# A paged-attention and convolution decoder layer: cache pages by indexed gathers, convolution taps on two other engines, half of the modulation moved behind the sample loop

## The reference, cut to what matters

```
mod = silu(c) @ w_ada + b_ada                 # 6 groups of 1024: sh1 sc1 gt1 sh2 sc2 gt2
h = rms_norm(x, g_norm1) * (1 + sc1) + sh1
q, k, v, glu_a, glu_b, gate_a, gate_c = split(h @ w_in)
q, k = rms_norm(q), rms_norm(k)               # per head
# each query: the 3 past blocks of 256 keys with the largest q . mean(k), and its own block
attn = moba_attention(q, [k_past, k], [v_past, v]) @ w_attn_proj
u = glu_a * sigmoid(glu_b)
cv = depthwise_conv([conv_past, u], w_dwconv) + b_dwconv     # 31 taps, 512 channels
cv = silu(layer_norm(cv)) @ w_conv_proj
x = x + gt1 * ((sigmoid(gate_a) * attn + sigmoid(gate_c) * cv) @ w_out)
h2 = rms_norm(x, g_norm2) * (1 + sc2) + sh2
y = x + gt2 * ((silu(f_g) * f_u) @ w_ffn_out),  f_g, f_u = split(h2 @ w_ffn_in)
```

## Time and profile before

| | |
|---|---|
| time, median of 3 runs | 642.4 us (642.4, 643.26, 638.41) |
| span of the profiled execution | 639.2 us |
| PE busy | 547.9 us, 86% |
| DVE busy | 459.7 us, 72% |
| ACT busy | 191.0 us, 30% |
| POOL busy | 84.0 us, 13% |
| DMA | 159.32 MB, mean 249 GB/s |
| the chain that ended last | PE 56%, DVE 30%, DMA 9% |

### The profile page before, as it was taken

One profiled execution on the slowest core, in us unless ns is written; L12 is line 12 of the kernel. 1 busy time (PEld: TensorE's weight loads), 2 busy tenths in 40 slices (PEclk: granted clock), 3 DMA queues, 4 the chain that ended last, 5 costly groups with the idle time before them and its releaser, 6 DMA issues.

```text
span 639.2 us, 11366 instructions
## 1 busy us (share of the span) xinstructions
PE 547.9 (86%) x4000; PEld 449.8 (70%) x4000; DVE 459.7 (72%) x851; ACT 191.0 (30%) x315; POOL 84.0 (13%) x176
## 2 busy tenths in 40 slices
PE   5779998685959597879758979978999999999997
PEld 3656676453545355555526678967999999999997
DVE  3325795999997999999997579866566656655541
ACT  1102213303030303030312455337444444433341
POOL 8101400022222222223222000000000000000000
PEclk9879999799888988979888989996999999999999
DMA  9998895498999899999949995542547455366600
GB/s 293 381 387 298 271 303 213 142 311 323 336 386 342 305 316 386 368 328 328 373 168 368 334 339 211 171 132 91 174 151 232 146 188 167 92 182 181 181 35 35
DMA packets 112234, 159.32 MB, mean 249 GB/s; under 512 B 6173, under 2 KB 67658, under 8 KB 112169
## 3 DMA queue, kind: packets, MB, share of 16 engines
q1 hardware_dynamic: 100722, 122.76, 58.3%
q0 software_dynamic: 10752, 34.16, 14.9%
q10 hardware_dynamic: 703, 1.67, 0.7%
HBM read 156.33 MB, written 2.72 MB: 249 GB/s over the span
## 4 chain that ended last, share of the span: by engine, by line
PE 56%; DVE 30%; DMA 9%; issue 2%; SPq 1%; ACT 1%; DVEq 0%; ACTq 0%
PE acc L1319 13%; PE acc L1320 12%; PE acc L1321 12%; PE acc L1134 11%; DVE prod L727 7%; DVE sall L734 7%; DMA wring<-in_w_ada 6%; DVE cvT L772 5%; DMA wring<-in_w_in 2%; PE acc L1101 1%; PE chain L1276 1%; DMA wring<-in_w_conv_proj 1%; PE acc L1092 1%; DVE wlo L972 1%; PE chain L1289 1%
## 5 line engine op out<-in xcount | busy, mean ns | idle before, releaser
L1134 PE MATMUL acc<-hT,wring 128*128 128x264 f32 x576 | 158.6, 429 | 3.7 <-DMA wring<-in_w_in 2.6
L972 DVE TENSOR_TENSOR wlo<-wring,whi 128x1024 fp32r<-128x1024 f32 (+2 forms) x92 | 101.8, 1108 | 70.2 <-ACT whi L449 69.0
L1134 PEld LDWEIGHTS acc<-hT,wring 128*128 128x128 f32 x576 | 116.3, 210 | 40.2 <-issue 15.8
L1319 PE MATMUL acc<-xlo,whi 128*128 128x264 f32 x416 | 122.6, 295 | 6.5 <-DVE xlo L978 5.9
L1320 PE MATMUL acc<-xhi,wlo 128*128 128x264 f32 x416 | 119.7, 288 | 0.0
L1321 PE MATMUL acc<-xhi,whi 128*128 128x264 f32 x416 | 119.6, 288 | 0.0
L449 ACT ACTIVATE whi<-wring 128x1024 fp32r<-128x1024 f32 (+2 forms) x92 | 88.6, 965 | 93.6 <-PE acc L1321 91.3
L271 POOL DMA_DIRECT2D vring<-in_cache_v x128 | 68.8, 537 | 257.7 <-PE chain L1276 140.2
L1319 PEld LDWEIGHTS acc<-xlo,whi 128*128 128x128 f32 x416 | 80.0, 192 | 9.1 <-issue 5.7
L1320 PEld LDWEIGHTS acc<-xhi,wlo 128*128 128x128 f32 x416 | 80.3, 193 | 0.2
L727 DVE TENSOR_TENSOR prod<-kring,qbc 128x1024 f32<-128x1024 f32 x64 | 77.2, 1206 | 3.8 <-PE qbc L1155 3.2
(11 more groups left out here) (200 smaller groups left out, 500.7 us busy)
## 6 DMA issues: line engine op xcount, KB each, us to landing
kring<-in_cache_k SPq DMA_DIRECT2D x128, 256.0 KB, 5.6
vring<-in_cache_v POOLq DMA_DIRECT2D x128, 256.0 KB, 6.1
wring<-in_w_ada SPq DMA_DIRECT2D x24, 1024.0 KB, 12.6
wring<-in_w_ffn_in SPq DMA_DIRECT2D x22, 1024.0 KB, 7.0
wring<-in_w_in SPq DMA_DIRECT2D x12, 1024.0 KB, 8.4
wring<-in_w_ffn_out SPq DMA_DIRECT2D x16, 704.0 KB, 6.0
wring<-in_w_in SPq DMA_DIRECT2D x12, 512.0 KB, 8.7
wring<-in_w_out SPq DMA_DIRECT2D x4, 1024.0 KB, 9.6
```

What stands on the lines that cost most here:

```text
L972: v.tensor_tensor(wlo[:, place, 0:n, :], w, whi[:, place, 0:n, :].bitcast(F32), ALU.subtract)\
L1134: ins = mm(bank[:, 0:R], w[:, k, P * t:P * t + P], src[:, k, :], start=k == 0, stop=k == KD - 1)
L1319: mm(bank[:, 0:R], whi[:, place, k - k0, :], lo[:, k, :], start=k == 0, stop=False)
```

## The change

**Pages.** The page-wise loads are gone from SP and POOL. POOL issues indexed gathers of 1 MB instead, 32 for K and 32 for V: partition p takes 4 rows (8 KB in one piece) of the page and row that `rowof` names. A partition so holds neighbouring keys of one page and not the same key of four pages, and the distances, the block sums (`halves`, `upper`) and `pen` are made for that layout; `diag` and `pen` become twice as wide. The first 12 gathers (K and V of sample 0, K of sample 1; 12.6 MB) are issued together when `ada3` has landed (`w_full[0] >= 64`); the others between POOL's additions.

**Taps.** For each tap ACT writes a product into `cprod`, a ring of 5 (`tap_products`), and POOL adds it to `cvT` (`add_taps`). There are 20 a loop iteration for b = 0 to 5, in parts of 6, 6 and 8, so that the convolution is complete in b = 6. Its sums and centring move to b = 6, its variance to b = 7, and `scale_rows` behind the loop. Tiles a1 and b1 are computed before the loop, a2 to b3 in the loop until b = 4.

**Modulation.** The loop holds no chunk. Chunks 4 to 7 are computed behind units 5, 11, 15 and 19, chunks 8 and 9 in the norm behind `o7`, chunks 10 and 11 behind units 31 and 39 (`f7` and `f15`). `SLOTS` follows.

```
-SLOTS = (["ada0", "ada1", "ada2", "ada3", "q", "k", "v", "glu"]
-         + ["mix0", "mod4", "mix1", "mix2", "mod5", "mix3", "mix4", "mod6", "mix5", "mix6", "mod7", "mix7"]
-         + ["mod8", "mod9", "mod10", "mod11", "conv", "attn", "out0", "out1"]
+SLOTS = (["ada0", "ada1", "ada2", "ada3", "q", "k", "v", "glu"] + [f"mix{n}" for n in range(B)]
+         + ["conv", "mod4", "attn", "mod5", "mod6", "out0", "mod7", "out1", "mod8", "mod9"]
+         + ["fin0", "fin1", "mod10", "fin2", "fin3", "mod11"] + [f"fin{n}" for n in range(4, FT // 2)]
...
+ADA_AFTER = {5: 4, 11: 5, 15: 6, 19: 7, FIRST_FFN + 7: 10, FIRST_FFN + 15: 11}
+ADT_AFTER = {7: 4, 13: 5, 17: 6, 21: 7, FIRST_FFN + 9: 10, FIRST_FFN + 17: 11}
...
+CONV_RING = 5
+CONV_LOOPS = 6
+CONV_PART = CT * (TAPS - 1) // CONV_LOOPS
+CONV_SPLIT = (6, 6, 8)
...
-        def load_pages(eng, ring, cache, full, b, c):
-
-            for g in range(PC * c, PC * c + PC):
-                page = eng.value_load(pages[0:1, bass.ds(PG * b + g, 1)], min_val=0, max_val=NPHYS - 1)
-                eng.dma_start(ring[:, g, :], cache[bass.ds(page, 1)].rearrange("o p h d -> p (o h d)"))\
-                    .then_inc(full[c], 16)
...
+            def gather(ring, cache, full, b, c):
+
+                g.indirect_dma_start(
+                    out=ring[:, PC * c:PC * c + PC, :].rearrange("p j n -> p (j n)"), out_offset=None,
+                    in_=cache.rearrange("n (r j) h d -> (n r) (j h d)", j=PC),
+                    in_offset=bass.IndirectOffsetOnAxis(ap=rowof[:, b, c:c + 1], axis=0)).then_inc(full[c], 16)
...
+            def add_taps(b, part):
+
+                for i in conv_part(b, part):
+                    t = i // (TAPS - 1)
+                    pool.wait_ge(prod_ready, i + 1)
+                    if i >= 1:
+                        pool.wait_ge(conv_added, i)
+                    g.tensor_tensor(cvT[:, t, 0:S], cvT[:, t, 0:S], cprod[:, i % CONV_RING, :], ALU.add)\
+                        .then_inc(conv_added, 1)
+
+            pool.wait_ge(rows_ready, 4)
+            pool.wait_ge(acc_full, NUMBER["vec"] + 1)
+            pool.wait_ge(w_full[0], 64)
+            for c in range(CH):
+                gather_k(0, c)
+            for c in range(CH):
+                gather_v(0, c)
+            for c in range(CH):
+                gather_k(1, c)
             for b in range(B):
...
+                for part in range(3):
+                    add_taps(b, part)
+                    if b + 2 < B:
+                        gather_k(b + 2, part)
+                if b + 1 < B:
+                    for c in range(CH):
+                        gather_v(b + 1, c)
+                if b + 2 < B:
+                    gather_k(b + 2, 3)
...
+            def tap_products(b, part):
+
+                for i in conv_part(b, part):
+                    t, n = i // (TAPS - 1), 1 + i % (TAPS - 1)
...
+                    if i >= CONV_RING:
+                        act.wait_ge(conv_added, i - CONV_RING + 1)
+                    func(cprod[:, i % CONV_RING, :], u[:, t, n:n + S], ACT.Copy, scale=taps[:, n, t:t + 1])\
+                        .then_inc(prod_ready, 1)
...
-                tap()
                 multiply_next(3)
-                tap(TAPS if b == B - 1 else 1)
                 add_up_next(3)
-                if b == B - 1:
-                    samples_convolution()
-                tap()
...
+            modulation(8)
             square_sum(KD - 1)
+            modulation(9)
+            mod_turned(8)
+            mod_turned(9)
```

351 lines of the change are left out of this document (168 added, 183 removed).

## The result

The changed kernel takes 684.3 us (682.84 to 687.03, 4 runs) beside 641.65 us of the kernel before: 1.0649 times, 95% interval 1.0592 to 1.0706. Forecast were 661 us and a range of 638 to 684, whose upper end it passes by 0.3. The profiled execution has a span of 685.3 us, 46.1 more than before, with a mean granted clock of 0.90 instead of 0.93.

What follows compares the result with a forecast made beforehand. DVE was taken to bound the sample loop, with DMA also full, and PE and DVE close behind it. Terms +8 + 7.5 - 18 - 7 + 28 = +18.5 on a 639.2 span made 657.7; 3.2 under the median gave 661 us, range 638 to 684.

Steps and rivals of the forecast that it cites:

- part 4's slots: Units from cp0 on: late weight slots make PE wait 5.2, 1.4 and 6.4 us, within a term of +28.
- The norm: Norm behind the output projection: chunks 8 and 9 and `norm_scale` ahead of the reciprocal add 3.4 us.
- The loop: Iterations b = 0 to 6: 28.8 us for four, 27.8 for two, 32.9 for the last; -18 in all.
- my 5 us: Iteration b = 6: the convolution's centring, small operations and a wait for the sums add 5 us.
- The tail: From b = 7 to the first unit: 33 us instead of 40.2, so -7.
- Before the loop: Pages and projections ahead of the loop: +8 for late q beside the gathers, +7.5 for two tiles, +15.5.
- The tiles: Tiles a1 and b1 ahead of the loop: 7.36 us of PE with no engine's work beside it, +7.5.
- the lower end: Before the loop: q's missing weights come at about 170 GB/s beside the gathers, the delay's low case, +4.
- (a): Before the loop: queue turns of four times the size delay q by 16 us, not 8: 669 us, chance 0.20.
- (b): Loop: POOL becomes the bound, 36 us in each of six iterations: +45, 706 us, chance 0.10.
- (c): Loop: iterations fall to DVE's 25.6 us: 638 us, or 626 with the units' ring waits hidden; chance 0.17.
- (d): Loop: DVE and POOL hinder one another and nothing is left of the loop's gain: 679 us, chance 0.08.

Runs made afterwards that it cites:

- e1: Changed kernel with another order of weight slots, chunks and unit weights alternating, chunk 4 between the loop and cp0: 659.2 us, 1.0234.
- e4: Changed kernel without the taps' products on ACT and additions on POOL: 681.7 us, one run.
- e13: Changed kernel with e6's, e7's and e12's edits, chunks 4 to 8 in the loop, 9 and 10 ahead of cp0, 11 in the feed-forward part: 644.7 us.
- e9: Kernel of e7 with the page table's transfer on ACT's queue instead of SP's, ahead of the weights: 686.6 us, one run.
- e12: Changed kernel with the page table loaded once into one partition and spread to 128 by a matmul: 684.1 us, one run.
- e6: Changed kernel with the first gathers issued when k's weights have landed, not when chunk 3 has: 679.8 us, one run.
- e15: Kernel of e13 with chunk 8 at the head of iteration 7 instead of in iteration 6: 640.4 us, 0.9996.
- e16: Kernel of e15 with tiles a1 and b1 in iteration 0 instead of ahead of the loop: 640.3 us, 0.9985.
- e7: Changed kernel with the operations that make the list of rows placed behind DVE's copies of x: 683.7 us, one run.

## Why the prediction was wrong

**The step that failed is part 4's slots.** "ap7 waits 5.2 [...] `out1` waits for chunk 6: +1.4 [...] `fin0` [...] stops o7: +6.4" named the right three loads and the right mechanism (e1 removes some 24 us by the order), and took each wait too short: 8.04, 4.41 and 10.59, 23.0 instead of 13.0. (They stand ahead of ap6, o2 and o6: a turned chunk takes a bank between, which the prediction had left out.) o7 ends 90.8 us after cp0's start and not 74. `out0`'s slot was free at t0 + 25.7, not 23.7, as cp0 started at a granted clock of 0.50. `out1` had waited for chunk 6, which itself came behind the first wait. For `fin0` I took 7.5 us to land, and it took 14.0, as chunk 9's 2 MB stood right ahead of it on the same queue. The other 7 of the 17 us are a term that the sum did not have: PE runs at a lower clock after each long wait, 0.85 over the stretch where e1 has 0.95, and is busy some 6 us longer for the same matmuls. The norm came near its term, +4.0 instead of +3.4.

**The loop** was forecast at 28.8 and 27.8 us and takes 28.4 to 29.4 in its middle; most of the miss is at its ends, 2.3 us in iteration 0 and 2.8 in iteration 6. The failed step is that the taps cost nothing once they leave DVE ("ACT adds 20 products of some 0.35 to 6 us of 31: hidden"). A product takes 0.50, DVE's two-input operations slow down beside the additions, and e4 gives the taps 6.2 us of the loop, 2.5 of it in iteration 0. In iteration 6 PE waits 4.66 us for ppad behind the centring, the mean clock is 0.72, and the values' product takes 6.23 instead of 3.64; neither the wait nor the clock was in my 5 us.

**The tail** was sized at 33 and is 34.4 to 36.6 in six profiles. Its cover was right: PE idles 8.21 us ahead of cp0, where e13 hides two chunks.

**Before the loop** the sum (15.5, measured 14.2) came out near by luck. The late q had been put down to gathers that share the engines. They were issued at 36.7, 3 us after I had them, and did not delay q: its weights and chunk 3 were late by the table's transfer in their queue, which the sum did not have (e9, e12), and chunk 3 ran at the low clock. q lost 3.2 us so and not 8, and the gathers cost k 2.7 (e6), for which I had nothing. The tiles cost more than they should, 9.1 instead of 7.4. One sum was wrong too: 1.55 MB at 170 GB/s are 9.1 us instead of 4.0, which makes the lower end +5 and not +4.

**The rivals.** (a): q1's share beside the gathers is 29% of the bytes, between the third that I took and the fifth of this rival, but it does not decide, as q's weights did not wait for the gathers. The rule of the Trainium skill, DMA: Bandwidth & Descriptors, Queues, rings and completion order, is that an engine takes a whole packet from each queue in turn. The profile counts 828 packets of some 7.4 KB on q0 and 1246 of 2.0 KB on q1. The page's packet holds several descriptors, and no run here shows how many of the profile's make one, so the trace neither confirms nor refutes the rule; the even count of the earlier trace rows did not carry over. (b) fell: a gather's 1.25 and an addition's 0.86 make 27 us in an iteration of 28.5, closer than thought, but POOL is busy only 21.63 of them, and inside iteration 1 it waits for ACT's products (0.86 and 1.93 us), not they for it. (c) fell, iterations stay above 28. (d) is right in kind and too large in size. DVE's multiply, with its query in PSUM, is spared, as the prediction said: 1210 ns on average and 1206 before. But the operations with both inputs in SBUF slow down beside the additions, `ppad` from 284 to 486 ns in the median and up to 606, and e4 takes the cost away. It is some 5 us of DVE's time in six iterations, where (d) gave away the whole gain of 18. The trace so agrees with the rule of the Trainium skill, GPSIMD Engine Reference, Specifications, that POOL shares its way to SBUF with DVE and the two contend when a DVE instruction has two SBUF inputs.

**Did the idea fail?** Freed of its slot order, its table and its late chunks, the changed kernel is level with the kernel before (e15, e16), no better. By e15's stages the loop gives 9.7 us and the tail 4.3, and they pay for 11.1 before the loop (the two tiles, the gathers and their list), 0.9 in the units and 3.3 behind them, where chunk 11 stands. I found no version that is clearly faster than the kernel before.

## What to carry to other kernels

In a ring of few slots the price of an insertion is not its bytes but whose slot the next load takes over: write down for each load its predecessor, when that is read for the last time, and add the landing time as it is *beside the traffic of that stage* (7.5 us in one stage, 22.7 in another). If the sum is later than the consumer, reorder, so that what is read once and what is held long alternate. An engine that prefetches ahead of its own work stops everything behind it when the prefetch is late, and PE pays for a long stop again with a slow start (cp0's first 25 matmuls at a clock of 0.50). And work taken from a bound engine shortens the loop only down to the chain between the engines: 5.9 us of taps an iteration left DVE for 2.5 us of period. It is not free on the engines it moves to either: POOL's additions made DVE's two-input operations slower.

## What the runs showed that I had not expected

- 64 KB (128 pieces of the same 512 bytes) in front of the weights on SP's queue cost the weights 1.5 us of all 16 engines' work; the same transfer on ACT's queue cost them nothing (e9).
- POOL's additions of 128x256 stretched DVE's 128x128 product of two SBUF inputs from 284 to 486 ns in the median, and left its 128x1024 multiply with one input in PSUM alone.
- A queue that held pages for 32 partitions of 8 KB each, and weights, moved 183 GB/s at a share of 84.6%, where pages on 128 partitions moved at 387.
- A gather of 1 MB with one index per partition costs POOL 0.95 us, 1.25 to the next, not much more than a plain page's 0.54 and 1.14.
- In e9 and e12 the end of chunk 3 reached ACT and SP 4.6 us after PE's last matmul by the profile (releaser "remote"), and at once in the changed kernel, e7 and e13. I have no cause for it.
